# One half-unit of gate work moves ahead of the second value product in every chunk of the mixer

## The reference, cut to what matters

```
proj = xn @ w_in            # mq mk mv mo mi mf aq ak av gt
h_m  = h_m * rsqrt(mean(h_m * h_m) + EPS) * g_mhead     # per head, h_m from the chunked mLSTM
h_m  = h_m * sigmoid(mo)
p    = exp(scores - mx);  out = (p / denom) @ v         # attention over a window of 128 keys
mixed = sigmoid(ga) * (h_m @ w_a) + sigmoid(gb) * (h_a @ w_b)
x = x + mixed @ w_out;  x = x + conv_ffn(rmsnorm(x))
```

## Time and profile before

| | us |
|---|---|
| median of 3 runs | 2935.09 (2933.42 to 2937.05) |
| the profiled execution, its own time | 2935.02 |
| its span, first to last instruction | 2933.2 |
| PE busy in the span | 2878.6 |
| DVE, ACT, POOL busy | 1772.3, 1375.8, 660.6 |
| the prompt's chunks in the mixer, about | 450 to 1038 |

### The profile page before, as it was taken

One profiled execution on the slowest core, in us unless ns is written; L12 is line 12 of the kernel. 1 busy time (PEld: TensorE's weight loads), 2 busy tenths in 40 slices (PEclk: granted clock), 3 DMA queues, 4 the chain that ended last, 5 costly groups with the idle time before them and its releaser, 6 DMA issues.

```text
span 2933.2 us, 43596 instructions
## 1 busy us (share of the span) xinstructions
PE 2878.6 (98%) x16354; PEld 2752.2 (94%) x16354; DVE 1772.3 (60%) x2545; ACT 1375.8 (47%) x2376; POOL 660.6 (23%) x942
## 2 busy tenths in 40 slices
PE   8999999999999999999999999999999999999998
PEld 8888789989988989999999999999999999999997
DVE  4222167666767657655587655876557765577665
ACT  3221235444555445545465444654446544455454
POOL 2111111212111212112242122321213322134232
PEclk9999999999999999999999999999999999999999
DMA  5343256656645464543434544345443455334434
GB/s 168 126 133 101 92 192 184 191 151 210 221 159 160 131 205 117 169 133 110 151 106 156 159 140 150 110 145 163 138 154 115 139 156 149 117 114 122 133 116 94
DMA packets 248275, 423.92 MB, mean 145 GB/s; under 512 B 38850, under 2 KB 162178, under 8 KB 248066
## 3 DMA queue, kind: packets, MB, share of 16 engines
q1 hardware_dynamic: 245954, 421.00, 46.0%
q10 hardware_dynamic: 2112, 0.13, 0.0%
HBM read 356.31 MB, written 65.77 MB: 144 GB/s over the span
## 4 chain that ended last, share of the span: by engine, by line
PE 63%; DVE 1%; ACT 0%; issue 0%; DVEq 0%; ACTq 0%
PE f_ps L1965 42%; PE f_ps L1970 21%; PE f_st L1977 0%; DVE f_rinv L2193 0%; DVE both_low L2315 0%; ACT f_wh L2027 0%; DVE f_wl L2172 0%; DVE both_high L2197 0%; DVE f_xl L2206 0%; DVEq L2428 0%; ACT L2036 0%; ACT f_rinv L2036 0%; ACT f_xh L2065 0%; DVE both_low L2307 0%; ACT f_hh L2057 0%
## 5 line engine op out<-in xcount | busy, mean ns | idle before, releaser
L2172 DVE TENSOR_TENSOR f_wl<-both_high,f_wh 128x1024 fp32r<-128x1024 f32 (+2 forms) x460 | 544.2, 1183 | 142.9 <-ACT f_wh L2027 137.4
L1965 PE MATMUL f_ps<-f_xh,f_wh 128*128 128x416 f32 x1760 | 618.1, 351 | 3.0 <-DVE f_xl L2206 3.0
L1965 PE MATMUL f_ps<-f_xl,f_wh 128*128 128x416 f32 x1760 | 618.6, 351 | 0.0
L2027 ACT ACTIVATE f_wh<-both_high 128x1024 fp32r<-128x1024 f32 (+2 forms) x460 | 442.0, 964 | 288.3 <-PE f_ps L1970 287.9
L1970 PE MATMUL f_ps<-f_xh,f_wl 128*128 128x416 f32 x1760 | 367.9, 351 | 0.0
L1965 PEld LDWEIGHTS f_ps<-f_xh,f_wh 128*128 128x128 f32 x1760 | 330.1, 188 | 10.5 <-DVE f_xl L2206 4.7
L1965 PEld LDWEIGHTS f_ps<-f_xl,f_wh 128*128 128x128 f32 x1760 | 330.9, 188 | 3.9 <-issue 0.6
L2225 DVE SCALAR_TENSOR_TENSOR both_high<-both_high,f_taps 128x416 f32<-128x416 f32 (+2 forms) x264 | 154.3, 598 | 296.7 <-ACT both_high L2085 296.5
L1970 PEld LDWEIGHTS f_ps<-f_xh,f_wl 128*128 128x128 f32 x1760 | 329.9, 188 | 2.3
L2083 ACT ACTIVATE both_high<-f_ps 128x416 f32<-128x416 f32 (+2 forms) x264 | 116.8, 460 | 390.3 <-PE f_ps L1970 390.2
L743 PE MATMUL pp<-gxh,gwh 128*128 128x416 f32 x792 | 292.2, 369 | 5.2 <-DVE gxl L699 5.2
(11 more groups left out here) (317 smaller groups left out, 5007.5 us busy)
## 6 DMA issues: line engine op xcount, KB each, us to landing
both_high<-in_w_up SPq DMA_DIRECT2D x220, 512.0 KB, 3.7
both_high<-in_w_dn SPq DMA_DIRECT2D x120, 384.0 KB, 3.0
both_low<-in_w_gate SPq DMA_DIRECT2D x80, 512.0 KB, 4.7
both_high<-in_w_br SPq DMA_DIRECT2D x40, 512.0 KB, 3.9
both_high<-in_w_out SPq DMA_DIRECT2D x40, 512.0 KB, 3.6
gate_rows<-gsgo SPq DMA_DIRECT2D x98, 208.0 KB, 3.1
proj_rows<-both_high SPq DMA_DIRECT2D x12, 900.0 KB, 4.5
both_low<-in_w_mix SPq DMA_DIRECT2D x20, 512.0 KB, 5.3
```

The costliest lines, as they stand in the source:

```text
L1965: pe.matmul(ps[n][:, 0:TB], wh[s][:, (col + k) * P:(col + k) * P + P], x[:, k0 + k, :], start=(k == 0 and x is xhi), stop=False)
L2027: act.activation(wh[v % WS][:, 0:w], raw[s][:, 0:w], ACT.Copy).then_inc(ev("w_hi"), 1)
L2172: dve.tensor_tensor(wl[n][:, 0:w], raw[s][:, 0:w], wh[n][:, 0:w].bitcast(F32), ALU.subtract).then_inc(ev("w_lo"), 1)
```

## The change

`SLOTS` becomes six places, 1, 3, 1, 1, 3 and 2 halves. The half of the old place 5 stands at the end of place 4, on every engine; the old place 6 is now called 5, with the same two halves. So on PE the second value product, the head's transposes and the next chunk's transposes follow one another. `LAST_STATE`, the place at which SP stores the final state in the last chunk, goes from 5 to 4. No instruction is added or taken away. The sample stage (`LATE`, seven places) is as it was.

```
-SLOTS = (1, 3, 1, 1, 2, 1, 2)
+SLOTS = (1, 3, 1, 1, 3, 2)
-LAST_STATE = 5
+LAST_STATE = 4
@@ PE @@
             units_pe(pe, n, 4)
             mix_pe_pv(pe, n, q, 1)
-            units_pe(pe, n, 5)
             mix_pe_hm(pe, n, q)
             if n < N:
                 mix_pe_tr(pe, n + 1, 1 - q)
-            units_pe(pe, n, 6)
+            units_pe(pe, n, 5)
@@ DVE @@
             mix_dve_h3(dve, n, q)
-            units_dve(dve, n, 5)
             if n < N:
                 mix_dve_low(dve, n + 1, 1 - q)
             if n == GATED_B:
                 gated_dve(dve)
-            units_dve(dve, n, 6)
+            units_dve(dve, n, 5)
@@ ACT @@
             units_act(act, n, 4)
             mix_act_ha(act, n, q, 1)
-            units_act(act, n, 5)
             mix_act_hm(act, n, q)
...
-            units_act(act, n, 6)
+            units_act(act, n, 5)
```

## The result

| | before | changed |
|---|---|---|
| median of 5 runs, us | 2935.09 | 2963.99 |
| lowest, highest | 2933.42, 2937.05 | 2961.11, 2970.61 |
| profiled execution, its own time | 2935.02 | 2961.85 |
| its span | 2933.2 | 2960.1 |

The ratio is 1.0102, 95% interval 1.0091 to 1.0113: the kernel is 1% slower. Single runs lie 9.5 us apart where they lay 3.6 apart before; part of that spread turns out to be in the mechanism, though the kernel before also spread over 7.9 us in the 27 runs beside the later experiments. The page of the profile hardly shows where the time went: PE is busy for 2881.8 us where it was for 2878.6, and DVE, ACT and POOL have nothing more to do than before (1768.4, 1377.9 and 654.1 us; the earlier trace rows).

The account below looks back on a forecast made before the run. PE, busy for 98% of the span, was taken as the bound. Even chunks 18.7, n = 10 3.6, odd chunks 0, last chunk -0.3 and clock 11.2 sum to 33.2 us on 2935.02: 2968 us, range 2955 to 2977.

Parts of the forecast that it names:

- The bound: Whole kernel: PE is busy for 98% of the span, so whatever makes PE idle is lost in full.
- The even chunks: DVE's `unit_low`, waiting for ACT, delays the head's sum and `hm`; PE idles 2.67 us in seven chunks, 18.7 us.
- PE's own arrival: Even chunks: PE itself would reach the head's transposes at about 704.9, before `hm` at 707.65.
- Chunk n = 10: The moved half begins a span, so DVE also gets four `unit_x` subtractions: head transposes 3.6 us later.
- The odd chunks: DVE has no work at the moved half, so `hm` comes at the same moment: 0 us.
- The tight place: Odd chunks: PE's key transpose waits for `mix_act_ha`, queued behind ACT's unit; fits by tenths, taken 0, at most 2.4 us.
- The switch: PE returns to the gates once less per chunk, saving 0.3 us; in even chunks this vanishes in the wait.
- The clock: PE's idle time drops its clock to 0.50 in each even chunk: 1.4 us times 8, 11.2 us; bounds 0 and 13.6.
- The first, stalls without a fall: Even chunks: the waits for `hm` come but PE's clock stays; 2957 us, chance 0.2.
- the one with more loss: Odd chunks: clock falls there too, or the key's transpose waits for ACT; 2979 us, chance 0.08.
- The faster one: At `mix_pe_hm` in even chunks `hm` does not decide; PE saves 0.3 us x 16, giving 2930; chance 0.03.
- No difference: Even chunks lose about a microsecond, or the next chunk's waits shrink by as much; 2935 to 2941, chance 0.04.

Follow-up runs that it names:

- the partly filled kernel: Changed kernel plus one throwaway fp32 matmul on PE ahead of the `hm` wait in even chunks (three at n = 10): 2957.61 us, ratio 1.0078.

## Why the prediction was right

**The bound.** PE had no time to spare, and what made it idle was lost in full: right. The waits for `hm` grew by 26.4 - 3.2 = 23.2 us, and the partly filled kernel, without falls, lost 22.4.

**The even chunks.** `unit_low` stands ahead of the sum and waits for ACT: 2.67 us a chunk predicted, 2.68 in five of the eight and 2.70 in a sixth. The first, n = 2, was 3.15 and not told apart. Taking the way from `gwl` to PE from the odd chunk was the step that carried this. PE's own arrival, given as about 704.9, adds up to 705.1 as written, since the gap of 0.3 us there already holds the usual 0.19 from one matmul to the next; the wait of 2.72 us agrees with 704.9.

**Chunk n = 10.** 3.6 predicted, 3.65 measured. The wait itself is 4.5 us, beyond the 2.5 to 3.7 given as a sign: the 0.68 us of before and the 0.2 by which PE arrives earlier come on top.

**The odd chunks.** 0 predicted; -0.15 where the clock did not fall, as `hm` is shorter, which the prediction did not see. The tight place, PE's transpose of the key behind `mix_act_ha`, held in the changed kernel. The run with PE and ACT moved shows how near it is: a late store in front of ACT's unit cost 2.5 us there.

**The switch.** 0.3 us predicted, 0.11 measured, as the 0.2 us of idle time behind the value product does not depend on what follows it. In the changed kernel it is hidden by the wait, as predicted.

**The clock.** This term was mis-sized, and it makes the 4 us between forecast and median, which lies only 1 us above the forecast's lower end of 2963. It was 11.2 us, a fall in each of eight even chunks; the median lies 2963.99 - 2957.6 = 6.4 us above the kernel without such falls. One execution had three falls and another eight. The one with eight took 11.9 us more in its chunks than the partly filled kernel (622.5 against 610.6), 1.5 each, so the price of 1.4 was nearly right and the number was not. How many falls the median execution had is not known. The step that failed was to read one idle time of 2.43 us, followed by a fall, as a rule for all idle times near its length: of the seven waits of 2.7 us, two were followed by a fall in one execution and all seven in the other. The row was a weak one, too. Small matmuls of the sample stage followed that idle time, and the same trace shows a fall behind small matmuls with no idle time of more than 0.26 us (window of the kernel before):

```profile
430.10:436.70 6.60, 6.60 (x32) 6.04 (x30) 5.04 (x14) 0.83 (x6) 1.39 (x2) 0.51 0.25 70
```

In the 4.5 us ahead of that stretch PE was busy for 4.24, mostly with small products (L1356, 128*64 by 128x8; L1410, 32*64 by 32x129). The Trainium skill's page "TensorE: Matmul & The Clock Gate", section "Why this matters for your kernels", would have had none fall at a length of 2.7 us; the traces contradict it, as up to seven of seven did. The 4.5 us of n = 10 are long enough for a fall by that page, so its rule gave one fall there and not none, as the prediction has it; both executions had that fall. Why one wait of 2.72 us costs the clock and the next one, behind the same instructions, does not stays open.

**The rivals.** The first, stalls without a fall, is what the partly filled kernel gives, 2957.6 against the 2957 worked out. Of the one with more loss nothing came: no fall lies behind the short wait of an odd chunk, and there is no wait at L822. The faster one was excluded by the trace's 3.86 us idle ahead of `gwl`: DVE did not pass over the waiting instruction. No difference was excluded by the result.

## What to carry to other kernels

A piece of filler work that is moved on one engine takes its share on every other engine along; look there for an instruction that waits, and for what is queued behind it. Here a unit's preparation, which nobody needed for two units, stood in front of a chain that PE needed at once; moved behind that chain in odd chunks as well, it gave 0.1% with PE's order of before and 0.2% with the new one, instead of costing 1%. Filler work should be placed on each engine by that engine's own chain, and the places need not match.

## What the runs showed of the hardware that was not expected

Idle times of the same length, 2.7 us, between the same instructions were followed by a stretch at the lower clock in two of seven chunks in one execution and in all seven in another, mostly at 1.5 to 1.65 us each. That made 8.0 of the 10.5 us between two executions of one kernel. Three throwaway matmuls in the wait (2.84 us together) removed these falls, and so did one, which left 1.66 us idle. Throwaway products on PE made the kernel 5 to 7 us faster than leaving it idle. A fall also came with PE busy nearly throughout, behind small products (430 us in the kernel before). And DVE's `hm` took 0.89 us where a copy of POOL ran beside it and 0.69 where none did.
